# Last layer's feed-forward: high and low rows in one 512 column product, halves of a bank added by VectorE

## The reference

```python
def squared_relu_mlp(h, w1, w2):
    return jnp.square(jax.nn.relu(h @ w1)) @ w2
...
        x_new = x_new + gt2 * squared_relu_mlp(modulate(rms_norm_2(x_new, g_norm2[i]), sh2, sc2),
                                               ffn_w1[i], ffn_w2[i])
```

## Time and profile before

| what | value |
|---|---|
| median of 3 runs | 1999.79 us (1997.75 to 2000.44) |
| profiled execution | span 1997.4 us, 28947 instructions |
| TensorE matmuls busy | 1874.0 us (94%) |
| VectorE busy | 1178.0 us (59%) |
| ScalarE busy | 903.5 us (45%) |
| mean granted TensorE clock | 0.978 of full |

### The profile page before, as it was taken

How to read it: one execution, slowest core, us unless ns; L and a number is a source line. 1 busy time by engine, 2 the same in 40 slices (tenths; PEclk the granted TensorE clock), 3 DMA queues, 4 the chain that set the end, 5 groups by cost and what they waited for, 6 DMA issues and landing times.

```text
span 1997.4 us, 28947 instructions
## 1 busy us (share of the span) xinstructions
PE 1874.0 (94%) x11398; PEld 1493.4 (75%) x11398; DVE 1178.0 (59%) x2039; ACT 903.5 (45%) x1552; POOL 104.1 (5%) x156
## 2 busy tenths in 40 slices
PE   7989889898999899999999999999899899998999
PEld 7859854444877654688887888888778548998999
DVE  5657653233723456669886766666743555666665
ACT  6454332123662667732334432232374676445543
POOL 0000002221000000000100000001000000000000
PEclk9979899999999999999999999999999999998999
DMA  9616699999442102046634444555633013544553
GB/s 327 210 38 207 223 377 403 402 402 393 142 148 85 37 1 84 23 157 201 211 130 144 147 140 155 165 193 197 203 100 106 22 43 118 179 157 151 178 190 127
DMA packets 210823, 345.48 MB, mean 173 GB/s; under 512 B 13760, under 2 KB 158400, under 8 KB 209408
## 3 DMA queue, kind: packets, MB, share of 16 engines
q1 hardware_dynamic: 188592, 284.88, 41.3%
q0 software_dynamic: 21952, 57.97, 8.4%
q10 hardware_dynamic: 144, 0.79, 0.1%
HBM read 392.86 MB, written 1.05 MB: 197 GB/s over the span
## 4 chain that ended last, share of the span: by engine, by line
PE 77%; DVE 8%; DMA 7%; ACT 5%; issue 3%; SPq 0%; DVEq 0%; ACTq 0%
PE PS L843 20%; PE PS L844 20%; PE PS L845 20%; DMA A<-in_w_exp 4%; PE PS L971 3%; PE PS L1181 2%; PE PS L987 2%; PE PS L999 2%; ACT CR L1402 2%; PE PS L977 1%; DVE CR L1825 1%; PE PS L1164 1%; DMA SCR<-in_w_exp 1%; PE PS L1209 1%; DVE JUNK L2124 1%
## 5 line engine op out<-in xcount | busy, mean ns | idle before, releaser
L1825 DVE TENSOR_TENSOR CR<-ring,CR 128x1024 fp32r<-128x1024 f32 x328 | 400.3, 1222 | 330.4 <-ACT CR L1402 319.8
L843 PE MATMUL PS<-HX,CR 128*128 128x256 f32 (+1 forms) x1512 | 508.1, 336 | 25.8 <-DVE HX L1874 11.4
L844 PE MATMUL PS<-HX,CR 128*128 128x256 f32 (+1 forms) x1512 | 497.8, 329 | 0.0
L845 PE MATMUL PS<-HX,CR 128*128 128x256 f32 (+1 forms) x1512 | 497.5, 329 | 0.0
L1402 ACT ACTIVATE CR<-ring 128x1024 fp32r<-128x1024 f32 x328 | 344.5, 1052 | 268.8 <-PE PS L845 266.9
L843 PEld LDWEIGHTS PS<-HX,CR 128*128 128x128 f32 x1512 | 291.9, 193 | 60.5 <-issue 34.5
L843 PE MATMUL PS<-AR,CR 128*128 128x256 f32 (+1 forms) x960 | 318.4, 332 | 8.5 <-DVE AR L1937 8.5
L845 PE MATMUL PS<-AR,CR 128*128 128x256 f32 (+1 forms) x960 | 317.7, 331 | 0.0
L844 PE MATMUL PS<-AR,CR 128*128 128x256 f32 (+1 forms) x960 | 317.6, 331 | 0.0
L844 PEld LDWEIGHTS PS<-HX,CR 128*128 128x128 f32 x1512 | 291.9, 193 | 28.6 <-issue 4.6
L845 PEld LDWEIGHTS PS<-HX,CR 128*128 128x128 f32 x1512 | 291.7, 193 | 24.2
(11 more groups left out here) (263 smaller groups left out, 2399.9 us busy)
## 6 DMA issues: line engine op xcount, KB each, us to landing
ring<-in_w_in SPq DMA_DIRECT2D x66, 1024.0 KB, 5.3
ring<-in_ffn_w SPq DMA_DIRECT2D x64, 1024.0 KB, 5.4
LC<-in_w_mod POOLq DMA_DIRECT2D x48, 512.0 KB, 4.1
BR<-in_w_mod POOLq DMA_DIRECT2D x48, 512.0 KB, 3.7
A<-in_w_exp SPq DMA_DIRECT2D x14, 1536.0 KB
HXW<-in_w_exp SPq DMA_DIRECT2D x12, 1536.0 KB
ring<-in_w_out SPq DMA_DIRECT2D x12, 1024.0 KB, 4.8
ring<-in_w_exp SPq DMA_DIRECT2D x8, 1536.0 KB
```

Source lines behind the costliest of these rows:

```text
L843: pe.matmul(bank, wh, xh, start=start, stop=False, skip_group_check=skip)
L844: pe.matmul(bank, wh, xl, start=False, stop=False, skip_group_check=skip)
L845: return pe.matmul(bank, wl, xh, start=False, stop=stop, skip_group_check=skip)
L1825: dve.tensor_tensor(lo, src, hi, ALU.subtract).then_inc(lo_done, 1)
```

## The change

In the last layer (l = 1) the high and the low rows become one operand of 512 columns, in two runs of 256 (`HX[:, :, k, 0:S]`, or `hidden_both`). The high weights are multiplied with it in one product that fills a bank: the left half holds high x high, the right half high x low. The low weights x high rows go into the right half too. So each weight slice has two products instead of three, and the halves have to be added afterwards. In an up tile VectorE does this with a `tensor_reduce` over pairs into `TMP`, multiplies the sum with its maximum with 0 into `SQ`, and ScalarE only copies `SQ`, rounded, into the high part. In a down tile VectorE adds gate x half to `X` twice. The first layer is unchanged.

```diff
         def up(g):
-            plan.fm([f"{L}up{g * GT + j}" for j in range(GT)], t["ffn_w1"][l][:, g * D:g * D + D], "act")
+            plan.fm([f"{L}up{g * GT + j}" for j in range(GT)], t["ffn_w1"][l][:, g * D:g * D + D], "dve" if l else "act")
...
+        def hidden_both(g, j):
+
+            at = (g % 2) * 2 * GT * 512
+            return AR[:, at:at + 2 * GT * 512].rearrange("p (s n) -> p s n", s=2)[:, :, j * 512:j * 512 + S]
...
+            def both_product(bank, w, x, k, last):
+
+                wh, wl = w
+                pe.matmul(bank.rearrange("p (s n) -> p s n", s=2), wh, x, start=(k == 0), stop=False)
+                return pe.matmul(bank[:, S:2 * S], wl, x[:, 0, :], start=False, stop=last)
+
+            def fm3_both(tile, x):
+
+                bank = open_tile(tile)
+                W = split_weights()
+                for k in range(KD):
+                    mm = both_product(bank, [w[:, k, :] for w in W], x(k), k, k == KD - 1)
+                mm.then_inc(tile_ready, 1)
+
+            def fm3_first_both(tiles):
+
+                banks = [open_tile(tile) for tile in tiles]
+                W = [split_weights() for _ in tiles]
+                for k in range(KD):
+                    pe.wait_ge(normed, waits.pop(0))
+                    for bank, w in zip(banks, W):
+                        mm = both_product(bank, [part[:, k, :] for part in w], HX[:, :, k, 0:S], k, k == KD - 1)
+                        if k == KD - 1:
+                            mm.then_inc(tile_ready, 1)
...
                 def up(g):
-                    if g == 0:
+                    if g == 0 and l:
+                        fm3_first_both([f"{L}up{j}" for j in range(FIRST)])
+                    elif g == 0:
                         fm3_first([f"{L}up{j}" for j in range(FIRST)], T)
                     for j in range(0 if g else FIRST, GT):
-                        fm3(f"{L}up{g * GT + j}", T)
+                        if l:
+                            fm3_both(f"{L}up{g * GT + j}", lambda k: HX[:, :, k, 0:S])
+                        else:
+                            fm3(f"{L}up{g * GT + j}", T)
...
                     for j in range(KD):
-                        fm3(f"{L}down{g}_{j}", T, lambda k: hidden(g, k, T))
+                        if l:
+                            fm3_both(f"{L}down{g}_{j}", lambda k: hidden_both(g, k))
+                        else:
+                            fm3(f"{L}down{g}_{j}", T, lambda k: hidden(g, k, T))
...
                         n = FFN // P * l + g * GT + j
+                        if l:
+                            act.wait_ge(hid_sq, n + 1)
+                            act.activation(hidden(g, j, T)[0], SQ[:, j % 2, 0:T], ACT.Copy).then_inc(hid_hi, 1)
+                            continue
...
+                def residual_both(name, j, tile, last):
+                    ps, x, gate = bank(name), X[:, j, 0:S], MOD[:, l, tile + j, 0:1]
+                    step(dve.scalar_tensor_tensor(out=x, in0=ps[:, S:2 * S], scalar=gate, in1=x, op0=ALU.mult, op1=ALU.add))
+                    dve.scalar_tensor_tensor(out=x, in0=ps[:, 0:S], scalar=gate, in1=x, op0=ALU.mult, op1=ALU.add
+                                             ).then_inc(freed["dve"], 1)
+                    if last:
+                        own(name)
+                        c["x"] += 1
+                        dve.nop().then_inc(x_ready, 1)
...
                         split(name)
+                        if l:
+                            ps, y = bank(name), TMP[:, j % 2, 0:S]
+                            if g * GT + j >= 2:
+                                dve.wait_ge(hid_ready, hid0 + g * GT + j - 1)
+                            dve.tensor_reduce(y, ps.rearrange("p (s n) -> p n s", s=2), AX.X, ALU.add
+                                              ).then_inc(freed["dve"], 1)
+                            own(name)
+                            dve.scalar_tensor_tensor(out=SQ[:, j % 2, 0:S], in0=y, scalar=0.0, in1=y, op0=ALU.max,
+                                                     op1=ALU.mult).then_inc(hid_sq, 1)
+                            if j:
+                                rest(j - 1)
+                            continue
...
-                        residual(f"{L}down{g}_{j}", j, 40, last=g == GROUPS_F - 1)
+                        if l:
+                            residual_both(f"{L}down{g}_{j}", j, 40, g == GROUPS_F - 1)
+                        else:
+                            residual(f"{L}down{g}_{j}", j, 40, last=g == GROUPS_F - 1)
```

## The result

The changed kernel takes 2020.76 us (median of 4 runs, 2019.96 to 2024.09) against 2000.01 (4 runs); the ratio is 1.0109, 95% interval 1.0098 to 1.0121. It is slower by 21 us. The sign is as forecast, the amount two thirds of it: 32.4 was forecast, 21.5 was the first rival, the plain reduce.

The account below looks back on a forecast made before the run. TensorE bounds the last feed-forward; the change closes a VectorE-ScalarE circle longer than its tile. From 1999.8 us: 19.8 + 17.0 - 4.9 + 0.5 = +32.4, giving 2032.2 us; range 2018 to 2050.

Parts of the forecast that it names:

- circle: Up tiles: reduce, multiply, copy, high part, low part, next reduce wait in turn; Q + 3.10 us against TensorE's 2.77.
- the forecast's own factor: Time per length of the up tiles' reduce: each 0.1 us more was to add 3.2 us to the total.
- Q: Duration of VectorE's new reduce of the two halves in an up tile; taken as 1.03 us, bounds 0.69 and 1.87.
- rival 1: Plain reduce in the up tiles: only the count of values matters, Q = 0.69; +21.5 us, 2021.3; chance 0.30.
- rival 2: Dearer reduce in the up tiles, Q from 1.15 to 1.87, as pairs lie 1 KB apart; 2036 to 2059; chance 0.20.
- slice step: TensorE's two products per weight slice: 0.2267 + 0.120 = 0.3467 us instead of 0.360, saving 6.8 us over 512.
- free tiles: Tiles outside the held-up stretches: the 46 from tile 18 on are 0.107 us cheaper each, 4.9 us back.
- the first run: The 16 up tiles in a row: tile 18 starts at 1881.26 instead of 1861.51, a loss of 19.8 us.
- two short runs: Two later runs of 8 up tiles: each loses 8.5 us, 17.0 together (11.6 with the plain reduce).
- the rule for tile t+3: Three chunk buffers: tile t+3 starts on TensorE no earlier than reduce t's start + Q + 3.33 us.
- rival 3: The up tiles' circle stays hidden, as buffers bridge each run; only the products' saving remains, 1993.5 us; chance 0.05.
- Rival 4: The 512 column product, with rows in two runs, takes more than 0.24 us; some 3.4 us more in down tiles.

Follow-up runs that it names:

- probes: The changed kernel with 18 small reduces of unneeded values, from SBUF and PSUM, added on VectorE at the end of the program; 2028.42 us, a single time.
- down_only: The changed kernel with its up tiles as before, so only the down tiles have the new form; 1997.39 us, ratio to before 0.9993.
- high_first: The changed kernel, with ScalarE making the next weight chunk's high part ahead of its copy, not behind it; 1994.94 us, ratio to before 0.9978.
- the side by side rows: high_first with the high and low rows of a slice next to each other, so the 512 columns are one contiguous run; 1995.35 us, ratio to before 0.9979.
- low_last: The changed kernel, with VectorE taking the low part behind the reduce and multiply, ScalarE's order kept; 1996.76 us, ratio to before 0.9990.

## Why the prediction came out as it did

**The mechanism was right.** The circle is there, link by link. The sum gave Q + 3.10 us, so 3.79 with the plain reduce; measured 3.72. It costs in the up tiles only, it goes when it is opened at either end, and a longer circle costs more by the forecast's own factor.

**The term that was mis-sized is Q**, in the step "Two small reduces read with a stride ... I take 1.03". Measured 0.68 us. The rows were read rightly and carried to where they don't hold, in two respects: `probes` gives the same pattern its excess from SBUF and none from PSUM, and pairs have no excess even in SBUF. Either alone would have made 1.03 too much. The prediction had said that no row shows PSUM read with a stride, and named this as what speaks for rival 1. Rival 1's 2021.3 is the measured time within 0.6 us; that it is so close is in part luck, as the smaller errors below cancel. At 32 us of time for 1 us of Q, the 0.35 us too much are 11.2 of the 11.4 us by which the forecast was too high.

The rule on PSUM lines of the Trainium skill (Advanced Engine Details and Errata, "PSUM Cachelines"), cited with rival 2, isn't borne out for VectorE: 0.39 and 0.66 us from PSUM with strides of 32 and 30 values, and 0.68 us for the kernel's own pairs 256 apart, are what contiguous values take. What it says of matmuls was not tried.

**Two smaller errors hid each other.** The multiply takes 0.42 us, not the 0.48 of a residual. The residual reads PSUM and has a scalar per partition; the multiply has neither. PSUM isn't it: the norm's `scalar_tensor_tensor` (L1916), from SBUF alone and with a scalar per partition, takes 0.48 us as well. That leaves the scalar, or that both inputs are the same `y`; but a `tensor_tensor` with two different inputs (L2504) takes 0.42, so the scalar is the likelier cause. The shorter multiply takes 0.06 us off the circle, about 2 us in all. And the slice step is 0.353 us for much of the execution, not 0.3467, so that the free tiles give back 1.3 us less.

**The parts.** In the changed kernel tile 18, the last that the first run holds up, starts at

```profile
1875.13 0.47 PE L866 MATMUL PS<-AR,CR 128*128 128x512 f32 x1 [0.67 <-DVE CR L1867]
```

against 1861.51: 13.6 us lost (19.8 forecast, 14.3 with the plain reduce). The two short runs, ten tiles each with what they hold up, take 33.1 us (1892.15 to 1925.24, and 1941.97 to 1975.00) instead of 28.8: 8.5 us together, for which the forecast's terms give 14.9 and, plain, 9.4. The other 26 tiles give back 1.5 us (2.8 forecast). Together 20.6 us until TensorE's end, and the last residual adds 0.5: 21.1, by a span that grew by 21.2.

**Smaller steps.** Down tiles: hidden, as said. Where VectorE has to catch up, its low parts follow one another 2.05 us apart in down tiles (1873.76, 1875.81, 1877.86; 2.06 forecast), and the residual of tile 20 is the first that waits for TensorE again (1883.87), as forecast. `down_only` can't be told from before by its time, and TensorE waits for no low part in it. TensorE waits for the low part ahead of the 16 tiles from the fourth to tile 18, and of six in each short run (28 by the starts; the view of waits counts 27), as the rule for tile t+3 has it. The clock stayed. That the circle stays hidden (rival 3) is out. Rival 4 is right in so far as the longer step exists and takes half of the products' saving where it lasts; but it comes with contiguous rows as well.

## What to carry to other kernels

Ahead of moving work between two engines that run in order, draw who waits for whom through one round of the loop: if each has, ahead of the operation that the other needs, one that needs the other, the sum of the round bounds the loop, whatever the busy shares say. The cure can be free: here one line that lets ScalarE do what it can already do first turned +1.1% into -0.2%, and no version of the study was faster. A price read in one memory, or for one pattern, isn't the price in another; where the forecast hangs on it, keep the plain one as the first rival. And one profiled execution can't tell a pace that is the program's from one that this execution happened to have.

## What the runs showed of the hardware

- TensorE has two rhythms for a pair of a 512 and a 256 column product, 0.3467 and 0.3533 us, at the same granted clock of 1.00. `high_first` kept the long one throughout in both executions, the side by side rows the short one in one and the long one in the other. In `low_last` it is the short one from the fourth tile until about 1945 us and the long one after. Over 512 slices the difference is 3.4 us. In every profile with the new form in all tiles, the step of one tile differs from that of the tile before only where TensorE started the tile late: in the changed kernel among the tiles that wait for a low part, in `low_last` at 1945.19, a product that starts 0.28 us after the one before it instead of 0.12. From then on the step stays until the next late start. What makes it come out short or long there stays open; nothing was tried on it.
- VectorE's reduce over groups with a stride takes from SBUF 0.14 us more than from PSUM for 224 values (groups of 7, 32 apart), and for 496 (groups of 16, 31 apart) 0.35 us more than the contiguous price, which PSUM keeps to at 480 values. Pairs 255 apart cost nothing extra in SBUF (0.68 us), nor do pairs 256 apart in PSUM (0.68). Why pairs are free wasn't tried.
- VectorE's `scalar_tensor_tensor` on 256 fp32 values takes 0.48 us with a scalar per partition, whether it reads PSUM (L2370, L2371) or SBUF alone (L1916), and 0.42 with a constant and one input read twice (L2515).
